# Prompt attention of a hybrid decoder step: value splits in six rotating places, key splits in five, query splits later, another order of the value products

## The reference, cut to what matters

```python
def fox_prompt(q, k, v, logf):                     # set 0
    s = jnp.einsum('bqhd,bkhd->bhqk', qb, k).astype(jnp.float32) * scale
    s = s + cb[..., :, None] - c[..., None, :]
    p, _ = softmax_stats(s, kpos[None, :] <= qpos[:, None])
    return jnp.einsum('bhqk,bkhd->bqhd', p.astype(v.dtype), v)
...
    for g in range(N_GROUPS):                      # sets 1 to 3: windows 128, 512, 2048, dilations 1, 4, 16
        o, lse = dilated_prompt(q, k, v, window, dilation)
...
def merge_groups(outs, lses):
    a = jax.nn.softmax(jnp.stack(lses, 0), axis=0)
    return jnp.einsum('gbsh,gbshd->bshd', a.astype(o.dtype), o)
```

## Time and profile before

| what | value |
|---|---|
| median of 3 runs | 1852.18 us (1850.48 to 1853.21) |
| the profiled execution | 1851.22 us |
| its span | 1849.4 us |
| mean granted TensorE clock | 0.978 |
| PE busy over the span | 1731.7 us (94%) |
| prompt attention | from about 1104.5 to 1305 us |
| in 1100 to 1310 us (210 us) | PE 168.01, ACT 160.47, DVE 147.77, POOL 122.35 us busy; clock 0.92 |

### The profile page before, as it was taken

How to read it: one execution, slowest core, us unless ns; L and a number is a source line. 1 busy time by engine, 2 the same in 40 slices (tenths; PEclk the granted TensorE clock), 3 DMA queues, 4 the chain that set the end, 5 groups by cost and what they waited for, 6 DMA issues and landing times. The chain is left out here.

```text
span 1849.4 us, 32331 instructions
## 1 busy us (share of the span) xinstructions
PE 1731.7 (94%) x10749; PEld 1539.9 (83%) x10749; DVE 1088.6 (59%) x2482; ACT 958.0 (52%) x1644; POOL 872.5 (47%) x508
## 2 busy tenths in 40 slices
PE   7999999999889999999999967888897999999998
PEld 5787877899878898889889846778796989899897
DVE  5746456422298888888888877777443433424151
ACT  5434343432257887878878867888323312222130
POOL 1515243300138878778778747665231333333231
PEclk9999999999899999999999988999899999999999
DMA  7284666644699999999999876320535565665752
GB/s 229 92 290 172 231 235 213 189 138 118 200 311 353 330 344 358 337 342 337 341 349 344 299 229 163 81 69 1 174 130 204 205 250 228 271 250 227 272 214 110
DMA packets 190955, 426.72 MB, mean 231 GB/s; under 512 B 24201, under 2 KB 85514, under 8 KB 189394
## 3 DMA queue, kind: packets, MB, share of 16 engines
q1 hardware_dynamic: 185330, 414.24, 64.5%
q10 hardware_dynamic: 2304, 8.39, 1.7%
q0 software_dynamic: 3168, 2.11, 0.5%
HBM read 392.36 MB, written 119.59 MB: 277 GB/s over the span
## 5 line engine op out<-in xcount | busy, mean ns | idle before, releaser
L1060 POOL TENSOR_TENSOR vv_lo<-v_raw,vv_hi 128x1024 fp32r<-128x1024 f32 x178 | 400.5, 2257 | 147.2 <-ACT vv_hi L1143 140.9
L1903 POOL TENSOR_TENSOR w_lo<-w_raw,w_hi 128x2048 fp32r<-128x2048 f32 x39 | 180.7, 4635 | 337.8 <-ACT w_hi L1918 337.8
L1135 ACT ACTIVATE kt_hi<-ktp 128x1024 fp32r<-128x1024 f32 (+1 forms) x192 | 186.1, 969 | 106.5 <-PE ktp L1322 105.5
L1162 DVE TENSOR_TENSOR kt_lo<-ktp,kt_hi 128x1024 fp32r<-128x1024 f32 (+1 forms) x192 | 221.0, 1151 | 5.5 <-ACT kt_hi L1135 3.7
L1336 PE MATMUL s_ps<-kt_hi,q_st 128*128 128x256 f32 (+3 forms) x768 | 205.1, 301 | 4.5 <-DVE mx_parts L1215 4.2
L1322 PE MATMUL ktp<-ident,k_raw 128*128 128x128 f32 x1440 | 192.5, 276 | 10.9 <-DVEq L1150 6.2
L1322 PEld LDWEIGHTS ktp<-ident,k_raw 128*128 128x128 f32 x1440 | 168.4, 142 | 37.1 <-issue 8.1
L696 PE MATMUL acc<-w_hi,xn_hi 128*128 128x512 f32 x480 | 195.0, 406 | 2.4 <-POOL w_lo L335 2.4
L1143 ACT ACTIVATE vv_hi<-v_raw 128x1024 fp32r<-128x1024 f32 (+1 forms) x192 | 191.3, 997 | 6.6 <-PE o_ps L1352 5.2
L696 PE MATMUL acc<-w_lo,xn_hi 128*128 128x512 f32 x480 | 190.6, 397 | 0.0
L1336 PE MATMUL s_ps<-kt_lo,q_st 128*128 128x256 f32 (+3 forms) x768 | 190.2, 281 | 0.0
(11 more groups left out here) (243 smaller groups left out, 4182.3 us busy)
## 6 DMA issues: line engine op xcount, KB each, us to landing
k_raw<-in_cache_fox_k SPq DMA_DIRECT2D x256, 256.0 KB, 6.1
v_raw<-in_cache_fox_v SPq DMA_DIRECT2D x256, 256.0 KB, 5.3
out_win_kv_sample<-in_cache_win_kv SPq DMA_DIRECT2D x32, 2040.0 KB, 9.5
w_raw<-in_w_in SPq DMA_DIRECT2D x32, 1024.0 KB, 5.9
k_raw<-in_cache_win_kv SPq DMA_DIRECT2D x40, 512.0 KB, 10.0
v_raw<-in_cache_win_kv SPq DMA_DIRECT2D x40, 512.0 KB, 10.6
w_raw<-in_w_up SPq DMA_DIRECT2D x16, 1024.0 KB, 5.3
w_raw<-in_w_down SPq DMA_DIRECT2D x16, 1024.0 KB, 5.1
```

Of the source, the lines that this page charges most:

```text
L1060: gp.tensor_tensor(vv_lo[:, slot, 0:tiles, :], v_raw[:, i % RAW_RING, 0:tiles, :], vv_hi[:, slot, 0:tiles, :].bitcast(F32), ALU.subtract). ...
L1135: act.activation(kt_hi[:, slot, :, 0:n], ktp[:, i % 2, :, 0:n], ACT.Copy).then_inc(k_hi, 1)
L1162: ve.tensor_tensor(kt_lo[:, slot, :, 0:n], ktp[:, i % 2, :, 0:n], kt_hi[:, slot, :, 0:n].bitcast(F32), ALU.subtract).then_inc(k_lo, 1)
L1903: gp.tensor_tensor(w_lo[:, slot, :], w_raw[:, slot, :], w_hi[:, slot, :].bitcast(F32), ALU.subtract).then_inc(slab_lo_done, 1)
```

## The change

- Values: `v_hi`/`v_lo` get six places instead of four. They are split in the order of the products: pieces w = 0 and 1 at ACT steps 27 and 28, w = 2 and 3 at 35 and 36 (POOL one step later). Raw values lie in slot 1 of `w_raw`; the slab that was there is loaded after the last pair's value split.
- Keys: five places instead of four, splits one step earlier (`K_AT` 12).
- Queries of the first head: split at steps 7 to 10 of their pair instead of 0 to 3 (steps 39 to 42 of the pair before), `q_lo` on POOL one step behind.
- Value products: places 0 to 3 take i % 4 = 2, 0, 1, 3 (set 1, FOX, set 2, set 3) for key tiles 0 to 2, and 1, 2, 3, 0 (FOX last) for key tile 3. The waits move with them. Set 2's first product is issued as two column halves.

```diff
-Q_AT, K_AT = (0, 18), 13
-V_HI_BEHIND, V_LO_BEHIND = 35, 36
+Q_AT, K_AT = (7, 18), 12
+K_RING, V_RING = 5, 6
+V_AT = (27, 28, 35, 36)
+WEIGH_ORDER = (2, 0, 1, 3)
+LAST_ORDER = (1, 2, 3, 0)
+def weighed_as(kt, w):
+    return LAST_ORDER[w] if kt == 3 else WEIGH_ORDER[w]
...
-            for n in range(2):
-                load_branch_slab(sp, a, w_raw, slab_loaded, n)
+            load_branch_slab(sp, a, w_raw, slab_loaded, 0)
...
+            sp.wait_ge(v_split, pieces(PAIRS - 1, SETS - 1))
+            load_branch_slab(sp, a, w_raw, slab_loaded, 1)
...
# keys_hi (ACT)
-                    done(act, scored, at_chunk(p, 28 + j) - CHUNKS)
+                    done(act, scored, at_chunk(p - 1, 28 + j - 1) if j else at_chunk(p - 2, 28 + SETS - 1))
# values_hi (ACT)
-                    done(act, weighed, at_chunk(p, i) - SETS)
+                        old = SETS * p + w - V_RING
+                        if old >= 0:
+                            done(act, weighed, at_chunk(old // SETS, 28 + LAST_ORDER.index(WEIGH_ORDER[old % SETS])))
# turns_hi (ACT)
-                done(act, weighed, at_chunk(p, i) - CHUNKS // 2)
+                done(act, weighed, at_chunk(p, i - i % 4 + (LAST_ORDER if i % 16 >= 12 else WEIGH_ORDER).index(i % 4)) - CHUNKS // 2)
# outputs (ACT)
+                at = at_chunk(p, i)
+                i += LAST_ORDER[i % 4] - i % 4
...
-                done(act, weighed, at_chunk(p, i))
+                done(act, weighed, at)
# weigh (PE)
+                    place = i % 4
+                    i += weighed_as(kt, place) - place
+                    w = WEIGH_ORDER.index(i % 4)
...
-                        pe.wait_ge(v_split, pieces(p, i % 4))
-                    if i % 4 < 2 and kt == 0:
-                        pe.wait_ge(o_copied, 4 * p + 2 * hh + kind + 1)
+                        pe.wait_ge(v_split, pieces(p, w))
+                    begins = kt == 0 and (kind == FOX or w == FIRST_WIN)
+                    if begins:
+                        pe.wait_ge(o_copied, 4 * p + 2 * hh + (2 if kind == FOX else 1))
                     done(pe, turned_lo, at_chunk(p, i))
```

More of the change, by code:

```diff
@@ L1419, in attend_prompt @@
         q_lo = sb("q_lo", [P, 2, SETS, SEQ], F32R)
[L1420 to L1423, removed]
+        k_hi = sb("k_hi3", [P, K_RING, SEQ], F32R)
+        k_lo = sb("k_lo3", [P, K_RING, SEQ], F32R)
+        v_hi = sb("v_hi3", [P, V_RING, Q_TILES, P], F32R)
+        v_lo = sb("v_lo3", [P, V_RING, Q_TILES, P], F32R)
         probs = sb("probs3", [P, s_cols])
@@ L1553, in split_lo, with values_lo, stage @@
                     gp.wait_ge(k_split_hi, pieces(p, j))
[L1554 to L1560, removed]
+                    slot = k_slot(p, j)
+                    gp.tensor_tensor(k_lo[:, slot], k_raw[:, s], k_hi[:, slot].bitcast(F32), ALU.subtract).then_inc(k_split, 1)
+            def values_lo(w):
+                def stage(p, i):
+                    if i == 0:
+                        gp.wait_ge(v_split_hi, pieces(p, w))
+                        slot, s = v_slot(p, w), value_set(w)
+                        gp.tensor_tensor(v_lo[:, slot], v_raw[:, s], v_hi[:, slot].bitcast(F32), ALU.subtract).then_inc(v_split, 1)
+                return V_AT[w] + 1, stage
             def normalise(p, i):
@@ L1588, in _ @@
             gp.tensor_copy(o_all[:, :, SEQ:N_TOK], o_t[:].rearrange("p k q n -> p (k q) n"))
-            straight(PAIRS, CHUNKS, (0, diagonals), (RECIP_BEHIND, normalise), (1, split_lo), (V_LO_BEHIND, values_lo))
+            straight(PAIRS, CHUNKS, (0, diagonals), (RECIP_BEHIND, normalise), (1, split_lo), *(values_lo(w) for w in range(SETS)))
         @block.scalar
@@ L1603, in split_inputs @@
                     act.wait_ge(k_in, 16)
-                    act.activation(k_hi[:, s], k_raw[:, s], ACT.Copy).then_inc(first_hi, 1)
+                    act.activation(k_hi[:, k_slot(0, i)], k_raw[:, s], ACT.Copy).then_inc(first_hi, 1)
                 for hh in range(2):
@@ L1664, in _ @@
                 ve.wait_ge(first_hi, 2 * j + 2)
-                ve.tensor_tensor(k_lo[:, s], k_raw[:, s], k_hi[:, s].bitcast(F32), ALU.subtract).then_inc(first_lo, 1)
+                ve.tensor_tensor(k_lo[:, k_slot(0, j)], k_raw[:, s], k_hi[:, k_slot(0, j)].bitcast(F32), ALU.subtract).then_inc(first_lo, 1)
             ve.wait_ge(in_small, N_SMALL)
@@ L1741, in score @@
                 for n, (q, k) in enumerate(((q_hi, k_hi), (q_lo, k_hi), (q_hi, k_lo))):
-                    last = pe.matmul(s_ps[:, i % BANKS, 0:len(tiles) * P], q[:, hh, s, qt * P:(qt + 1) * P], k[:, s, cols], start=(n == 0), stop=(n == 2))
+                    last = pe.matmul(s_ps[:, i % BANKS, 0:len(tiles) * P], q[:, hh, s, qt * P:(qt + 1) * P], k[:, k_slot(p, i % 4), cols], start=(n == 0), stop=(n == 2))
                 last.then_inc(scored, 1)
@@ L1770, in tile_products @@
                     end = min(kt + 2, Q_TILES) if s == 1 else Q_TILES
-                    cols, at = slice(kt * P, end * P), pt_at[s] + kt * pt_step[s]
+                    at = pt_at[s] + kt * pt_step[s]
+                    parts = [(0, 2), (2, Q_TILES)] if kind == WIN and kt == 0 and w == FIRST_WIN + 2 else [(kt, end)]
                     for n, (v, x) in enumerate(((v_hi, pt_hi), (v_lo, pt_hi), (v_hi, pt_lo))):
-                        last = pe.matmul(o_ps[:, kind, cols], v[:, s, kt, :], x[:, at + kt * P:at + end * P], start=(i % 4 < 2 and kt == 0 and n == 0),
-                                         stop=(unit_ends(i) and kt == Q_TILES - 1 and n == 2))
+                        for lo, hi in parts:
+                            last = pe.matmul(o_ps[:, kind, lo * P:hi * P], v[:, v_slot(p, w), kt, :], x[:, at + lo * P:at + hi * P], start=(begins and n == 0),
+                                             stop=(unit_ends(i) and kt == Q_TILES - 1 and n == 2))
                     last.then_inc(weighed, 1)
```

24 lines of the change are left out of this document (16 added, 8 removed).

## The result

The changed kernel takes 1863.7 us (median of 4 runs, 1862.4 to 1866.4), the kernel before it, run beside it, 1851.3 us (1846.7 to 1853.2). The ratio is 1.0072, 95% interval 1.0050 to 1.0095: slower by 0.5 to 1%. The profiled execution has a span of 1860.6 us, 11.2 more than before.

What follows compares the result with a forecast made beforehand. In the prompt attention PE was taken as busy 80% of the time, idling mostly in a few gaps per pair of heads; −0.4 −1.9 +3.7 +12.7 +2.3 −1.2 = +15.2 us gave 1866 us, range 1852 to 1875.

Steps and rivals of the forecast that it cites:

- Step 54: Second head's first value product: gap of 5.1 us instead of 1.59; +4.2 us each in pairs 0 to 2.
- the hold: On ACT, chunk 12 waits for the product ending step 37, as FOX is last in key tile 3; chunk 28 likewise.
- Step 38: First head's first value product: PE waits for chunk 14, new gap 3.5 us; −0.2 us each in pairs 1 and 2.
- The keys: Gap before a pair's first scores, 1.36 us: 0.4 taken back in three pairs, −1.2 us in all.
- Pair 3: Last pair: gap of 3.5 us at step 38, +3.7 us with the clock; 2.6 us at step 54, +2.3 us.
- Pair 0: First pair's step 38, where nothing holds chunk 12 back: −1.9 us (−3.4 to −0.5).
- The clock behind step 54: Lower clock after the longer gap at the second head's first value product: 1.4 us more in each of pairs 0 to 2.
- The Trainium skill: Its rule that brief, frequent PE idling loses clock would make the last pair's 2.6 us gap cost 1.4 us more.
- Queries at steps 39 to 42, the late slab and the halved columns: Each put at 0; queries up to +1 us a pair, the slab 5 us if its issue slipped to the end.
- The bounds: All terms' low ends together give about 1851 us, the high ends 1879.
- Rival (2): No change, 1851 us: step 54's gap grows by only 1 us in pairs 0 to 2 and the clock holds; chance 0.08.
- rival (1): Faster, 1839 us: the new wait for chunks 14 and 30 is a bare round of about 1.1 us; chance 0.11.

Runs made afterwards that it cites:

- e3: Changed kernel with the last key tile's value products in the order of before (FOX first again), the new order kept elsewhere: 1861.8 us.
- e4: Changed kernel with one wait replaced: a head's first value product waits for chunk 6 or 22 instead of chunk 14 or 30: 1848.1 us.
- e8: Changed kernel with the product order of before, no column halves, and the keys split from step 13 as before: 1836.1 us.
- e10: Changed kernel with the edits of e3 and e4 together: 1849.4 us.
- e1: Changed kernel with the product order of before and no column halves, moved splits and added places kept: 1832.7 us, run again 1832.8 us.
- e6: e1 with queries and keys split at the steps of the kernel before, values still moved with six places: 1843.7 us.

## Why the prediction came out as it did

The forecast was 1866 us, 1863.7 was measured, and the mechanism is the one it names. That the number came so close is in part luck: several terms were off and cancelled, as the list shows. To hold it against the trace step by step I compare stretches between first value products, since the gap, the clock behind it and the keys gap fall into different ones (before, after, difference, and what the terms of the sum give for it):

| stretch | before | after | diff | by the sum |
|---|---|---|---|---|
| start to pair 0, step 38 | 30.33 | 28.79 | −1.54 | −1.9 |
| to pair 0, step 54 | 24.11 | 26.83 | +2.72 | 3.5 − 0.4 = +3.1 |
| to pair 1, step 38 | 23.59 | 24.99 | +1.40 | 1.4 − 0.7 − 0.2 = +0.5 |
| to pair 1, step 54 | 24.15 | 26.84 | +2.69 | +3.1 |
| to pair 2, step 38 | 23.56 | 24.61 | +1.05 | +0.5 |
| to pair 2, step 54 | 24.18 | 26.86 | +2.68 | +3.1 |
| to pair 3, step 38 | 20.27 | 24.47 | +4.20 | 1.4 − 0.7 + 2.9 = +3.6 |
| to pair 3, step 54 | 18.88 | 21.93 | +3.05 | 1.4 − 0.7 + 2.6 = +3.3 |
| to the next phase | 16.89 | 16.71 | −0.18 | −0.3 |
| sum | | | +16.1 | +15.0 |

(The gap of step 54 and that of step 38 end the stretches named after them; the small gaps behind them that go, 0.28 and 0.40 and 0.69, and the clock count in the next stretch. The sum differs from +15.2 by rounding.)

- **Step 54**, the largest term: a gap of 5.1 us was forecast, 5.17 is measured in three pairs, ended by `pt_lo` of 128x256. One half-sentence of this step is wrong: that the hold stands in the way there as well. e3 takes the hold away and leaves 5.17; the queue of DVE sets the end with and without it.
- **Step 38** is the term that was mis-sized. The new gap is 4.0 us, not 3.5, and nothing made it good: the stretches give +0.7 and +0.6 us of idle time in pairs 1 and 2 where the sum had −0.2 each. From chunk 12's `pt_hi` to chunk 14's it is 3.47 us against the 3.17 summed, and PE starts 0.35 us behind `pt_lo`, where 0.15 was counted for all three hand-overs. Why it is 0.35 here and 0.10 at step 54 stays open. The second copy, which ends in between (1183.29 + 0.59 = 1183.88), does not explain it: in pair 0, before any copy is made, it is 0.26. In all traces with the new order the first head's product starts 0.25 to 0.35 us behind that `pt_lo` where it waits for it, the second head's 0.09 to 0.11 in pairs 0 to 2; the first head's also waits for `v_split`, and no run tries whether that is the reason. The cause was also drawn too simply, with everything of steps 36 to 38 behind the hold: without the hold (e3) 3.0 us are left, 1.0 less.
- **The keys** gave back 0.81 to 0.85 us a pair, not 0.4. That is 1.3 us in all, and nearly cancels the error of step 38 in pairs 1 and 2.
- **Pair 3**: 3.98 at step 38 against 3.5, and 2.18 at step 54 against 2.6. They cancel as well. **Pair 0** came out at −1.54 us against −1.9.
- **The clock behind step 54** was put at 1.4 us. The stretch to pair 1's step 38 has +0.68 us at its own gap and −0.68 for the small gaps that went, so that all of its +1.40 is the clock; the same for pairs 2 and 3 leaves 1.12 (1.05 − 0.61 + 0.68) and 1.46 (4.20 − 3.42 + 0.68). Behind the last pair's 2.18 us it held at 1.00, as the sum had it.
- **The Trainium skill**, "TensorE: Matmul & The Clock Gate", section "A second HAM failure mode: psum-queue depth-cycling", tells of a kernel whose PE idles so often for short times between groups of matmuls that its clock oscillates. The traces agree only in part. All six gaps of 2.3 us in e4 were followed by a lower clock, and the gaps of 1.35 and 1.59 us in two pairs of e8. The same two gaps left it at 1.00 in three pairs of the kernel before, and so did the 2.18 us of the changed kernel's last pair.
- **Queries at steps 39 to 42, the late slab and the halved columns** were put at 0. The timeline of the changed kernel shows no gap of PE at steps 39 to 42, and the one before the next phase is 8.52 us against 8.38 before, so the late slab cost nothing to speak of. The halves were not measured apart.
- **The bounds**: added up with pairs 1 and 2 as stated, the low ends give −1.9 us and the high ends +27.2, which is 1849 and 1878 us, not 1851 and 1879. Rival (2), at 1851, lies just outside the range that is said to take it in.
- **What the forecast did not see** is how much the good half is worth. Its rival (1) put the time at 1839 us if the new wait were a bare round; without the order, with nothing new to wait for at all, it is 1832.7. Both of the order's costs, and the splits' gain of 15.9 us of phase, went into one number.

## What to carry to other kernels

Look at a count that a reordered instruction waits for against what it reads: the count for a chunk produced in the same step cost 16 us of the phase here, and the data were there eight steps before. When one accumulator must be copied out before the next group begins, begin with the one that was finished first; the two other combinations tried here paid for the copy (e10) or for a hold and the copy (e4). And measure the parts of a bundle apart: here a bundle of 0.7% loss held a gain of 1%.

## What was not expected of the hardware

The clock is not decided by the length of a gap alone. e1 ran twice; both traces have a gap of 1.31 us in front of the first scores of pair 1. The first run's gap and the windows behind it:

```profile
1144.27 0.30 PE L1775 MATMUL s_ps<-k_hi,q_hi 128*128 128x128 f32 x1 [1.31 <-POOL k_lo L1579]
...
1145.00:1150.00 5.00, 4.79 (x42) 4.50 (x41) 4.21 (x13) 4.50 (x12) 3.94 (x3) 1.00 0.43 113
1150.00:1155.00 5.00, 3.24 (x19) 2.45 (x19) 4.81 (x15) 4.61 (x11) 1.13 (x2) 1.00 0.28 105
```

and the second's, with the gap itself:

```profile
1145.01 0.30 PE L1775 MATMUL s_ps<-k_hi,q_hi 128*128 128x128 f32 x1 [1.31 <-POOL k_lo L1579]
...
1145.00:1150.00 5.00, 4.97 (x29) 4.80 (x30) 3.89 (x10) 3.88 (x9) 4.69 (x3) 0.68 0.35 80
1150.00:1155.00 5.00, 5.00 (x28) 4.87 (x28) 4.78 (x17) 4.61 (x10) 0.39 (x1) 0.64 0.42 161
```

The same program, the same gap, and once the clock stays at its upper level (2.4 GHz), once it goes to the lower (1.2 GHz) for some microseconds. Over all these kernels every gap of 2.8 us and more in front of a value product was followed by a lower window, but for one: 3.10 us in e3's last pair left the clock at 1.00. Those of 1.3 to 2.4 us went either way: 1.93 us in e6 and 2.18 in the changed kernel without, 1.84 in e6 and 2.08 in the changed kernel with one. Gaps under 0.9 us mostly went without one, but not always (e8 has 0.66 in the window from 1275, with gaps of 0.87 and 0.76 us in a row). So a gap between 1.3 and 2.4 us had a price here that the gap's length did not decide.
